# Gates inside the q group, indexer blocks half a group earlier, and twelve low parts a layer on GpSimd, in a two-layer decoder trunk

## What is computed

```
sh1, sc1, g1, sh2, sc2, g2 = split(silu(c) @ w_mod + b_mod)       # 1024 x 6144
h = x * (1 + sc1) + sh1
q, k, v, qi, ki, wi, xr, yg = split(h @ w_in)                     # 512 each but ki (64), wi (8)
q, k, qi, ki = rotary(...)
# indexer: 8 heads of 64; score[t, s] = sum_h wi[t, h] * relu(qi[t, h] . ki[s]), causal
# attention: 4 heads of 128, over the 128 keys of each query with the largest score
# LRU: xc = causal depthwise conv of width 4 of xr
r, i = sigmoid(xc @ W_a + b_a), sigmoid(xc @ W_x + b_x)           # blocks of 64 x 64
a = exp(-8 r softplus(-lam));  u = sqrt(1 - a * a) * i * xc;  h_t = a_t h_(t-1) + u_t
lru = h * gelu(yg)
mix = concat(rms_norm(attention), rms_norm(lru)) @ w_out
x = layer_norm(alpha * x + (1 + g1) * mix)
ff = square(relu((x * (1 + sc2) + sh2) @ w_up)) @ w_down          # width 4096
x = layer_norm(alpha * x + (1 + g2) * ff)
```

## Time and profile before

| | |
|---|---|
| runs of the kernel | 1375.34, 1375.38, 1380.4 us; median 1375.38 us |
| the profiled execution, its own time | 1378.46 us |
| its span in the profile | 1376.8 us |
| PE busy | 1297.3 us, 94% |
| DVE busy | 803.4 us, 58% |
| ACT busy | 551.5 us, 40% |
| POOL busy | 98.7 us, 7% |
| mean granted clock of PE | 0.966 |

### The profile page before, as it was taken

How to read it: one execution, slowest core, us unless ns; L and a number is a source line. 1 busy time by engine, 2 the same in 40 slices (tenths; PEclk the granted TensorE clock), 3 DMA queues, 4 the chain that set the end, 5 groups by cost and what they waited for, 6 DMA issues and landing times.

```text
span 1376.8 us, 17026 instructions
## 1 busy us (share of the span) xinstructions
PE 1297.3 (94%) x6225; PEld 1019.5 (74%) x6225; DVE 803.4 (58%) x1322; ACT 551.5 (40%) x849; POOL 98.7 (7%) x107
## 2 busy tenths in 40 slices
PE   3999996889999999999999999878999999999996
PEld 2777773676888888888867767547868888888886
DVE  3647899556753734537465589975565334344353
ACT  3733536623631413324246345554264133242331
POOL 3100001002000000000120000100200000000012
PEclk8999998998999999999989999979989999999998
DMA  9763343211334253342245434410214332333221
GB/s 314 243 204 123 123 155 120 92 47 46 107 100 150 90 164 92 106 153 93 77 139 168 138 123 156 164 48 0 93 32 137 96 103 91 93 105 91 93 76 61
DMA packets 73397, 158.56 MB, mean 115 GB/s; under 512 B 6528, under 2 KB 10872, under 8 KB 73336
## 3 DMA queue, kind: packets, MB, share of 16 engines
q1 hardware_dynamic: 59904, 108.61, 25.2%
q0 software_dynamic: 12800, 48.76, 10.6%
q10 hardware_dynamic: 632, 0.39, 0.1%
HBM read 155.64 MB, written 2.10 MB: 115 GB/s over the span
## 4 chain that ended last, share of the span: by engine, by line
PE 83%; DVE 12%; DMA 2%; issue 2%; ACT 1%; POOL 0%; POOLq 0%; DVEq 0%; SPq 0%; ACTq 0%
PE bank L634 23%; PE bank L636 23%; PE bank L635 23%; DVE idx_acc L1593 3%; DVE best L1591 3%; PE bank L679 2%; DMA first_mod<-in_w_mod_dram 2%; DVE w_lo L1407 2%; PE bank L599 2%; PE bank L537 1%; PE bank L852 1%; PE bank L832 1%; PE bank L731 1%; DVE turned_ring L1544 1%; PE bank L889 1%
## 5 line engine op out<-in xcount | busy, mean ns | idle before, releaser
L1407 DVE TENSOR_TENSOR w_lo<-w_raw,w_hi 128x1024 fp32r<-128x1024 f32 (+1 forms) x216 | 237.6, 1114 | 360.4 <-ACT w_hi L968 360.4
L968 ACT ACTIVATE w_hi<-w_raw 128x1024 fp32r<-128x1024 f32 (+1 forms) x216 | 203.7, 960 | 493.5 <-PE bank L636 491.7
L634 PE MATMUL bank<-a_hi,w_hi 128*128 128x512 f32 x896 | 370.1, 413 | 9.1 <-DVE a_lo L1449 6.2
L635 PE MATMUL bank<-a_lo,w_hi 128*128 128x512 f32 x896 | 351.9, 393 | 0.0
L636 PE MATMUL bank<-a_hi,w_lo 128*128 128x512 f32 x896 | 351.6, 392 | 0.0
L634 PEld LDWEIGHTS bank<-a_hi,w_hi 128*128 128x128 f32 x896 | 169.6, 189 | 61.5 <-issue 24.2
L634 PE MATMUL bank<-b_hi,w_hi 128*128 128x512 f32 x512 | 199.7, 390 | 0.0
L636 PE MATMUL bank<-b_hi,w_lo 128*128 128x512 f32 x512 | 199.3, 389 | 0.0
L635 PE MATMUL bank<-b_lo,w_hi 128*128 128x512 f32 x512 | 199.2, 389 | 0.0
L635 PEld LDWEIGHTS bank<-a_lo,w_hi 128*128 128x128 f32 x896 | 169.9, 190 | 39.1 <-issue 3.8
L636 PEld LDWEIGHTS bank<-a_hi,w_lo 128*128 128x128 f32 x896 | 169.6, 189 | 36.6
(11 more groups left out here) (267 smaller groups left out, 1412.7 us busy)
## 6 DMA issues: line engine op xcount, KB each, us to landing
mod_raw<-in_w_mod_dram POOLq DMA_DIRECT2D x40, 1024.0 KB, 6.0
w_raw<-in_w_up_dram SPq DMA_DIRECT2D x64, 512.0 KB, 3.7
w_raw<-in_w_down_dram SPq DMA_DIRECT2D x64, 512.0 KB, 3.7
w_raw<-in_w_in_dram SPq DMA_DIRECT2D x48, 512.0 KB, 3.7
w_raw<-in_w_out_dram SPq DMA_DIRECT2D x16, 512.0 KB, 3.8
first_mod<-in_w_mod_dram SPq DMA_DIRECT2D x4, 1024.0 KB, 19.6
first_mod<-in_w_mod_dram POOLq DMA_DIRECT2D x4, 1024.0 KB, 15.3
x_in<-in_x_dram POOLq DMA_DIRECT2D x4, 512.0 KB, 15.0
```

The lines of the kernel that those rows point to most:

```text
L634: mm(o, wh, hi(kk), start=first, stop=False)
L635: mm(o, wh, lo(kk), start=False, stop=False)
L968: last = af(hi, src, ACT.Copy)
L1407: last = tt(lo, src, hi.bitcast(F32), ALU.subtract)
```

## The change

- `gate_pair(m)` runs ahead of steps 6, 12, 18 and 24 of group q instead of after yg. ACT's `gate_out(m)` follows in the order of the yg splits: high part 0, gates 0 and 1, high part 1, gates 2 and 3, high part 2, the copies of q, high part 3.
- Indexer block 1 goes into the second half of xr, block 2 into the first half of v, block 3 into the second half of v, none into k; the turn of wi goes ahead of step 15 of xr. The Relus, the adds and the convolution follow on ACT and DVE. The copies of xr come after the Relus of block 1.
- The low parts of q, yg and out0 (12 pairs a layer) are made by GpSimd. They stand behind the issue of the modulation loads 7 to 13. Each waits for a turn that DVE gives just before a run of rounds, for its high part and for the low part before it.
- DVE's rounds: up to 6, 12, 18, 22 and 23, then k's rotation, up to 26, 29, 32, 34, then q's rotation, up to 37, 39, 42, 45, then the attention loop. The LRU inputs are at u = 2 to 5 and the scans at u = 7 to 10 there.
- ACT's decay of tile m (Exp and Tanh) comes in the attention loop, behind unit m; the square roots after u = 6, the squares at u = 10 to 13.
- The gates, the LRU's root tile, the probabilities and the diagonal of the tokens lie in other places of SBUF. The diagonal of 1024 is no longer kept: two DVE operations of three operands multiply the identity instead, and two start-up instructions of GpSimd go.

The core of the diff:

```
+POOL_LO = ("q", "yg", "out0")
...
 # GpSimd
+                def low_part(name, p):
+                    g = group_at(name, l)
+                    pool.wait_ge(lo_turn, l * len(POOL_LO) * PAIRS + POOL_LO.index(name) * PAIRS + (p + 1))
+                    pool.wait_ge(hi_split, g * PAIRS + (p + 1))
+                    pool.wait_ge(lo_split, g * PAIRS + (PAIRS + p))
+                    gp.tensor_tensor(w_lo[:, p, :, :], raw[:, p, :, :], w_hi[:, p, :, :].bitcast(F32), ALU.subtract)\
+                        .then_inc(lo_split, 1)
+                lows_after = {7: lows[0:1], 8: lows[1:3], 9: lows[3:5], 10: lows[5:7], 11: lows[7:9], 12: lows[9:11], 13: lows[11:12]}
                 for n in range(LATE_PAIRS):
...
+                    for name, p in lows_after.get(n, ()):
+                        low_part(name, p)
...
 # PE
-                group("xr", l, a_high, a_low, nothing, between={HALF: lambda: late_mod(l, 2)})
+                group("xr", l, a_high, a_low, nothing, between={
+                    **dict(zip((19, 20, 22, 23, 25, 26, 28, 29), (idx_head(1, h) for h in range(IDX_HEADS)))),
+                    HALF - 1: turn_wi, HALF: lambda: late_mod(l, 2)})
...
                 group("v", l, a_high, a_low, nothing, between={
-                    **{2 * h + 1: idx_head(1, h) for h in range(IDX_HEADS)},
-                    **{HALF + 2 * h + 1: idx_head(2, h) for h in range(IDX_HEADS)}, HALF: lambda: late_mod(l, 4)})
+                    **{2 * h + 1: idx_head(2, h) for h in range(IDX_HEADS)},
+                    **{HALF + 2 * h + 1: idx_head(3, h) for h in range(IDX_HEADS)}, HALF: lambda: late_mod(l, 4)})
...
-                group("q", l, a_high, a_low, nothing, between={HALF: lambda: late_mod(l, 8)})
+                group("q", l, a_high, a_low, nothing, between={
+                    **{6 + 6 * m: gate_pair(m) for m in range(LT)}, HALF: lambda: late_mod(l, 8)})
...
 # DVE
-                for p, rounds_ in enumerate((4, 8, 13, 18)):
+                for p, rounds_ in enumerate((6, 12, 18, 22)):
+                    ve.sem_inc(lo_turn, 1)
                     topk(rounds_)
-                    idx_add(3, (2 * p, 2 * p + 1))
-                    if p < PAIRS - 1:
-                        split_lo("q", l, p)
...
-                topk(22)
-                slot(l, "yg", (k_out, lambda: topk(28), lambda: topk(34)))
-                topk(36)
-                slot(l, "out0", (q_out, lambda: topk(41), lambda: topk(45)))
+                topk(23)
+                k_out()
+                for p, rounds_ in enumerate((26, 29, 32, 34)):
+                    ve.sem_inc(lo_turn, 1)
+                    topk(rounds_)
+                q_out()
+                for p, rounds_ in enumerate((37, 39, 42, 45)):
+                    ve.sem_inc(lo_turn, 1)
+                    topk(rounds_)
...
-                    if u < LT:
-                        lru_input(u)
-                    elif 6 <= u < 6 + LT:
-                        lru_scan(u - 6)
+                    if 2 <= u < 2 + LT:
+                        lru_input(u - 2)
+                    elif 7 <= u < 7 + LT:
+                        lru_scan(u - 7)
...
 # ACT
+                def decay(m):
                     act.wait_ge(free_s[4], uses_before(4, f"gr{m}", l) + 1)
                     af(lru_a[:, m, :], th[:, m, :], ACT.Exp, scale=neg_sp[:, m:m + 1]).then_inc(decay_done, 1)
-                for m in range(LT):
                     act.wait_ge(decay_done, l * LT + (m + 1))
                     af(th[:, m, :], th[:, m, :], ACT.Tanh, scale=vcol("lru_lambda", m)).then_inc(lru_exp, 1)
...
+                    if u < LT:
+                        decay(u)
-                    if u == 5:
+                    if u == 6:
```

121 lines of the change are left out of this document (69 added, 52 removed).

## The result

The changed kernel takes **1366.7 us** (median of 13 runs, 1359.25 to 1369.82) against 1378.15 us (median of 13 runs, 1375.18 to 1380.4) before: ratio 0.9914, 95% interval 0.9896 to 0.9932. It is faster by 11.5 us, where 21 were predicted; 1354.4 us was forecast, and 1366.7 lies just outside the range of 1346 to 1366.

What follows compares the result with a forecast made beforehand. PE was taken as 94% busy, its winnable waits due to DVE's debt of top-k rounds carried into the attention. A gain of 10.5 us a layer, 21 in all, from 1375.38 gave 1354.4 us, range 1346 to 1366.

Steps and rivals of the forecast that it cites:

- Blocks forward: Indexer blocks half a group ahead: PE's work unchanged, group v ends about 7.9 us later, group k where it did.
- Gates into q: Gate products moved from before the scores into group q: 7.9 instead of 8.6 us of PE, a win of 0.7 us.
- Low parts on PE's path: Twelve low parts a layer on GpSimd, some 2.5 us each, were to put nothing on PE's path.
- DVE's schedule: DVE's rounds up to the attention: from 6 us late to about 4 us early at the first scores.
- the LRU inputs beside GpSimd's squares: Attention units: two DVE operations of up to 0.68 us per LRU input, with no cost for squares in the sum.
- a rival at 0.13: GpSimd's squares collide with LRU inputs: two inputs blocked by 1.25 us each, 8 us a layer, 1359.4 us; chance 0.13.
- The two-operand rotations pay about 0.5 us each time: DVE's rotations beside GpSimd's low parts: two meetings a layer, 1 us, inside DVE's 4 us.
- The first exponential: Start of the attention on ACT: first exponential at 222.1 us instead of 228.07, after one table load of 1.28 us.
- The pace of the units: Attention: ACT about 2.05 us a unit, DVE abreast; exponentials 3 to 6 at 228.5, 230.1, 231.8 and 233.5 us.
- From there PE is bound by its own work in both: From the scores of unit 13, at 250.0 instead of 260.47 us, PE's own work sets the time in both kernels.
- PE keeps its higher clock: Rival, chance 0.12: without the 5.9 us stop, products of the first six units shrink, 2 to 3 us more per layer, about 1349.
- only the first wait goes: Rival, chance 0.15: hand-offs between PE, DVE and ACT at PE's lower clock pace the units; only 6 us a layer, 1363.4.

Runs made afterwards that it cites:

- reordered: Changed kernel with q's, yg's and out0's fourth low parts on DVE, two more rounds before q's rotation, gate products behind round 46, spare PE products: 1358.52 us.
- the second profile: Profile of a repeat of the changed kernel with no edit, span 1357.5 us; the repeat's median was 1365.61 us.
- sums_apart: Changed kernel with the 32 one-column sums cut into four groups of eight around the turns of units 14 and 15: 1363.63 us.
- keep_busy: Changed kernel with 29 spare PE products a layer between the attention's units: 1360.81 us.
- reordered_apart: reordered with the 32 one-column sums in four groups: 1356.4 us.
- before_busy: Kernel before the change with spare PE products in its two long waits and between the units: 1374.39 us.

## Why the prediction was wrong, point by point

- **The baseline.** The forecast subtracted 21 from 1375.38, the median of three runs. Thirteen runs have their median at 1378.15. 2.8 of the 12.3 us of the miss are this; the profiled execution's own 1378.46 would have been the better base. The other 9.5 are gain that didn't come.
- **Blocks forward: right.** By themselves they bring 6.3 us, which was the larger half of the gain in the end.
- **Gates into q: right in size, useless in sum.** 0.8 us of PE a layer against 0.7. First scores at 222.0 and 221.2 us in the two profiles against 221.1. No gain in the median came of it.
- **Low parts on PE's path: right.** No wait for a low part shows; GpSimd took 2.4 to 2.8 us each against 2.5. The 2.5 was in part luck: it is twice a quarter of the 5.01 us of the earlier trace rows, and of those four squares three took 1.04 us and the last 2.02, held up by DVE as shown below.
- **DVE's schedule: half right.** It was to be 4 us early at the first row maximum and was 1.9. The prediction let two low parts fall into the rotations for 0.5 us each; they cost 2.05 and 2.20, and a third, not foreseen, 0.66. All of this stayed inside DVE's lead, so it cost no time by itself. "So the rounds are free" is right: MAX8 beside a low part stays at 0.69 us. That one-input operations of DVE don't conflict holds for MAX8 and MATCH_REPLACE8, but not for the mask: 0.69 instead of 0.43 us beside the squares.
- **The step that failed: the LRU inputs beside GpSimd's squares, put at nothing in the units.** The sum gives DVE "two operations of up to 0.68" for an LRU input, and no meeting with the squares. Measured: 1.52 and 1.48 us for two of the four first halves, 0.26 more for the mask, 1.9 us in layer 0 (1.7 in layer 1). The row maximum of unit 3 waits for it, and exponential 3 came at 230.5 us instead of 228.5, 3.7 behind the one before it: units further apart than 2.4 us were one of the prediction's signs of being wrong. It was a rival at 0.13, 2.5 us a layer; without the squares the units are 3.9 us shorter in both layers together than in the first profile, 2.6 than in the second, of 4.9 that were missing.
- **Why it was put at nothing: contention was mispriced.** "The two-operand rotations pay about 0.5 us each time" came from one DVE addition of 1.17 us. That was read as a price, but it was a remainder: GpSimd's instruction had begun at 310.89, 0.68 us ahead of DVE's, took 1.29 us, and the addition ended 0.55 us behind it. The rule that the prediction named, the Trainium skill, SBUF — State Buffer, Who interferes with whom, has a DVE instruction with two inputs in SBUF contend with a GpSimd one that reads SBUF; by that rule the meeting lasts as long as the other's instruction, and the trace agrees (2.88 us beside a low part of 2.69). The trace of the kernel before held a plainer case, 3 us behind the MAX8 row that the prediction quotes, DVE and then GpSimd:

```profile
226.27 1.56 DVE L1407 TENSOR_TENSOR w_lo<-w_raw,w_hi 128x1024 fp32r<-128x1024 f32 x1
```

```profile
226.71 2.02 POOL L500 TENSOR_TENSOR lru_a_squared<-lru_a 128x512 f32<-128x512 f32 x1
```

  DVE's low part takes 1.56 instead of 1.22 us behind the third square, and the fourth square 2.02 instead of 1.04 behind that low part.
- **The first exponential: right.** 223.16 and 222.33 us against 222.1, again 1.28 us of table load behind the last high part.
- **The pace of the units: right once the collisions are gone.** In reordered exponential 3 is at 228.4 us, as the sum had it.
- **"From there PE is bound by its own work in both": wrong.** Its work isn't of fixed length: the stage takes 20.4, 22.2 or 23.8 us by level. In the profiled execution it took 1.8 us more in each layer than before, in the second profile it took 1.6 less and 0.2 more. That the change makes it longer isn't shown; sums_apart speaks for the row of one-column sums, which both kernels have. The rival "PE keeps its higher clock" (0.12) thought only of the gain; the level that comes at another place and costs was in no case.
- **The rival "only the first wait goes"** (0.15, 1363.4 us) came nearest to the number. Its size fits: of the 7.1 and 7.6 us by which the units were shorter, 5.2 in each layer are the first exponential coming sooner behind the first scores. Its reason fits less: with the level held (keep_busy) only 1.0 and 1.4 us come back.

What stays open: why the gates' 0.8 us don't show, how the 4.9 us missing in the units divide between squares and level, and where PE's level falls in the executions of reordered_apart that are still 3 us apart.

## What to carry to other kernels

Work moved from DVE to GpSimd was free beside MAX8 and MATCH_REPLACE8, and was dear beside DVE's two-operand steps. Put the two queues side by side and price each such meeting at what is left of the other's instruction, up to the whole of it. A short row in which the two overlap is no price until you have seen when each began. Undoing each part of a change by itself shows which part carries it: here the modest one, blocks half a group forward, brought more than the twelve low parts that looked like the change. And a stretch of PE that is "bound by its own work" can have more than one length; here it was worth spreading 32 one-column products that stood in a row.

## What the runs showed of the hardware that was not expected

- One kernel's runs lay 10.6 us apart (1359.25 to 1369.82) with mean granted clocks of 0.975 to 0.966, and the two profiles of it differ in nothing but PE's level; with spare products in the waits the spread was 2.6 us over four runs (keep_busy), and 4.4 over twelve in the kernel before (before_busy).
- 32 one-column sums in a row, themselves 3.6 to 4.8 us, were followed in many executions by turns of 1.09 instead of 0.60 us and values of 1.9 instead of 1.06; in groups of eight between other products they were not (0.64 and 1.14 us in sums_apart).
- The wait for the other engine holds in both directions: DVE's multiplication of 0.68 us took 2.88 behind a low part of GpSimd, and GpSimd's square of 1.04 us took 2.03 behind a low part of DVE. A DVE mask with one operand took 0.69 instead of 0.43 us beside the squares.
